# Hybrid block of a two-model kernel: convolution turns moved into the projection, first tap on ScalarE, last heads transposed inside the output product, half of the gate's SiLU folded into an eviction

## The reference, cut to what matters

```python
def hybrid_mixer(h, w_in, conv_w, conv_b, dt_bias, a_log, d_skip, ssm_norm_g, fox_b_f, w_out):
    z, xbc, dt_raw, q, k, v, f_raw = jnp.split(h @ w_in, offs, axis=-1)   # 1024 | 1536 | 16 | 3 x 1024 | 8
    xbc = jax.nn.silu(causal_conv(xbc, conv_w, conv_b))                   # 4 taps, depthwise
    xs, bm, cm = jnp.split(xbc, [D_SSM, D_SSM + SSM_GROUPS * SSM_STATE], axis=-1)
    dt = jax.nn.softplus(dt_raw + dt_bias)
    y = ssd_chunked(xh, dt, -exp(a_log), bm, cm) + d_skip * xh            # 16 heads of 64
    y = y * jax.nn.silu(z)                                                # the gate
    y = y * lax.rsqrt(mean(y * y over each half of 512) + eps) * ssm_norm_g
    o = forgetting_attention(q, k, v, log_sigmoid(f_raw + fox_b_f))       # 8 heads of 128
    return jnp.concatenate([y, o], axis=-1) @ w_out                       # 2048 x 1024
```

## Time and profile before

| | |
|---|---|
| median of 3 runs | 1807.49 us (1804.84 to 1807.61) |
| the profiled execution, own time | 1804.47 us |
| its span in the profile | 1802.7 us |
| TensorE matmul busy | 1724.8 us (96%), 10448 instructions |
| VectorE busy | 1142.3 us (63%) |
| ScalarE busy | 907.1 us (50%) |
| mean granted TensorE clock | 0.98 of full speed |
| hybrid block in the span | about 895 to 1136 us |

### The profile page before, as it was taken

The page is one execution under the profiler, slowest core; times in us unless marked ns, Lnnn a source line. Parts: engine busy times, 40 slices in busy tenths (PEclk is TensorE's granted clock), DMA queues, the critical chain, the costliest instruction groups (busy, mean ns, idle before and its releaser), DMA issues. The chain is left out here.

```text
span 1802.7 us, 24492 instructions
## 1 busy us (share of the span) xinstructions
PE 1724.8 (96%) x10448; PEld 1424.2 (79%) x10448; DVE 1142.3 (63%) x1551; ACT 907.1 (50%) x1137; POOL 11.8 (1%) x25
## 2 busy tenths in 40 slices
PE   8899899998999999999999999999999999989998
PEld 7677688887867887888887777888888888768886
DVE  5786876667868767555666456754565556865554
ACT  5553544455344446443546644644464456954443
POOL 0000000000000000000000000000000000000000
PEclk9899999998999999999999998999999999999999
DMA  7222345442223554555544223655555555345553
GB/s 265 103 95 95 131 145 191 175 164 96 95 102 144 186 187 175 189 187 185 202 161 144 102 103 120 226 186 185 205 189 193 185 198 201 140 139 193 184 176 138
DMA packets 41597, 291.75 MB, mean 162 GB/s; under 512 B 4656, under 2 KB 4912, under 8 KB 7312
## 3 DMA queue, kind: packets, MB, share of 16 engines
q1 hardware_dynamic: 38880, 280.23, 43.3%
q0 software_dynamic: 2608, 9.96, 1.6%
HBM read 289.12 MB, written 1.05 MB: 161 GB/s over the span
## 5 line engine op out<-in xcount | busy, mean ns | idle before, releaser
L468 PE MATMUL pg<-wh,hTh 128*128 128x512 f32 (+1 forms) x2160 | 854.0, 395 | 23.2 <-DVE wl L1807 10.0
L1807 DVE TENSOR_TENSOR wl<-raw,wh 128x2048 fp32r<-128x2048 f32 x259 | 591.9, 2291 | 404.2 <-ACT wh L1242 401.7
L469 PE MATMUL pg<-wl,hTh 128*128 128x512 f32 (+1 forms) x2160 | 834.6, 386 | 0.0
L470 PE MATMUL pg<-wh,hTl 128*128 128x512 f32 (+1 forms) x2160 | 834.2, 386 | 0.0
L1242 ACT ACTIVATE wh<-raw 128x2048 fp32r<-128x2048 f32 x265 | 505.8, 1913 | 304.4 <-DMA raw<-weights 299.8
L468 PEld LDWEIGHTS pg<-wh,hTh 128*128 128x128 f32 x2160 | 410.5, 190 | 112.9 <-issue 16.7
L470 PEld LDWEIGHTS pg<-wh,hTl 128*128 128x128 f32 x2160 | 410.0, 190 | 82.6
L469 PEld LDWEIGHTS pg<-wl,hTh 128*128 128x128 f32 x2160 | 410.9, 190 | 74.9
L1333 ACT ACTIVATE arena<-pg,sm 128x512 f32<-128x512 f32 (+1 forms) x47 | 31.5, 669 | 191.1 <-PE pg L470 191.1
L2445 DVE SCALAR_TENSOR_TENSOR arena<-pg,sm,arena 128x512 f32<-128x512 f32 (+1 forms) x48 | 31.7, 702 | 33.9 <-PE pg L470 33.9
L1289 ACT ACTIVATE hTh<-ps 128x512 fp32r<-128x512 f32 x60 | 32.1, 594 | 38.1 <-PE ps L631 32.9
(11 more groups left out here) (375 smaller groups left out, 1147.9 us busy)
## 6 DMA issues: line engine op xcount, KB each, us to landing
raw<-weights SPq DMA_DIRECT2D x266, 1024.0 KB, 4.8
arena<-wide POOLq DMA_DIRECT2D x9, 512.0 KB, 3.6
x<-x_in SPq DMA_DIRECT2D x2, 512.0 KB, 6.3
cst<-const_tables POOLq DMA_DIRECT2D x1, 1024.0 KB, 5.3
plainh<-dist_tables POOLq DMA_DIRECT2D x2, 512.0 KB, 4.9
arena<-gate_mix POOLq DMA_DIRECT2D x1, 1024.0 KB, 6.2
arena<-token_mix POOLq DMA_DIRECT2D x2, 256.0 KB, 3.9
y_out<-x POOLq DMA_DIRECT2D x1, 512.0 KB, 2.9
```

Source lines behind the costliest of these rows:

```text
L468: pe.matmul(dst, lh, rh, start=first, stop=False)
L469: pe.matmul(dst, lh, rl, start=False, stop=False)
L470: return pe.matmul(dst, ll, rh, start=False, stop=last)
L1807: tt(wl[:, slot, :], raw[:, slot, :], wh[:, slot, :], ALU.subtract)\
```

## The change

Four things in the hybrid block:

1. The small product comes after the first projection block, and the first four groups of convolution transposes are issued inside the second and third projection blocks. `gemm`'s argument `inside` becomes a dictionary from (unit, chunk) to a function.
2. The last tap with the bias is made by ScalarE (`first_tap`, Identity with scale and bias), the other three by VectorE (`later_taps`).
3. The prepared chunks are dealt out anew (2, 10, 4, 2, 2, 3, then one for each SSD head but two at h = 8, 4 and 4; TensorE's attention loop keeps 16). ScalarE and VectorE take the last two chunks' work out of head 7.
4. At the end, group 3 of the attention output is turned inside the first output unit; ScalarE splits groups (0, 1), then a weight unit, then (2, 3); the SiLU of z is made for the first 512 columns by itself and for the last 512 as the function of the block's eviction; the gate's product is made by halves.

```diff
+        HYB_BLOCKS[-1] = HYB_BLOCKS[-1][:2] + (ACT.Silu,)
@@ TensorE
-                gemm(D, (512,) * 3, ("evac_act",) * 3, head=True)
+                def turned(g):
+                    def between():
+                        if g % 2 == 0:
+                            pe.wait_ge(sem["evac_act"], st.evacs["evac_act"])
+                        if g == 0:
+                            c.wait("small_read")
+                        if g >= 4:
+                            c.wait("conv_read")
+                        for j in range(2):
+                            for m in range(M):
+                                last = pe.transpose(...)
+                        last.then_inc(sem["conv_tr"], 1)
+                    return between
+                gemm(D, (512,), ("evac_act",), head=True)
                 small_gemm(24)
-                c.wait("small_read")
-                pe.wait_ge(sem["evac_act"], st.evacs["evac_act"])
-                for g in range(6):
-                    if g == 4:
-                        prepare(3)
...
-                prepare(7)
+                gemm(D, (512,) * 2, ("evac_act",) * 2, inside={(1, 1): turned(0), (1, 2): turned(1), (2, 2): turned(2),
+                                                               (3, 0): turned(3)})
+                prepare(2)
+                for g in (4, 5):
+                    turned(g)()
                 prepare(10)
...
-                    prepare(1)
+                    prepare(2 if h == 8 else 1)
...
-                c.wait("fox_read")
-                transpose_groups(o3, (3,), 0)
-                out_halves()
+                def last_heads():
+                    c.wait("fox_read")
+                    transpose_groups(o3, (3,), 0)
+                out_halves(last_heads)          # called in out_half after chunk 1 of the first unit
@@ ScalarE
+                gemm(D, (512,), ("evac_act",), read(0))
                 c.wait("gate_abs")
...
-                for n in (3, 7, 10):
-                    prepare(n)
+                pump(st.used + 4)
+                first_tap(0)
+                first_tap(1)
+                gemm(D, (512,), ("evac_act",), read(1))
+                first_tap(2)
+                first_tap(3)
+                gemm(D, (512,), ("evac_act",), read(2))
+                plan_blocks(HYB_BLOCKS)
+                prepare(2)
+                for g in (4, 5):
+                    first_tap(g)
+                prepare(10)
...
+                    if h < 7:
                         prepare(1)
                         prepare(1)
                 c.wait("fox_done", 2)
-                split_groups(range(4), 0)
+                split_groups((0, 1), 0)
                 pump(st.used + 3)
-                act.wait_ge(sem["evac_act"], st.evacs["evac_act"])
-                act.activation(HYB_Z, HYB_Z, ACT.Silu).then_inc(sem["z_ready"], 1)
-                pump(st.used + 4)
-                c.wait("o_sq")
+                split_groups((2, 3), 0)
+                act.activation(z3[:, :, 0:512], z3[:, :, 0:512], ACT.Silu).then_inc(sem["z_ready"], 1)
+                prepare(2)
+                pump(st.used + 3)
+                # squares: o_sq is waited for ahead of each half
@@ VectorE
+                pump(st.used + 4)
+                later_taps(0)
+                later_taps(1)
+                gemm(D, (512,), ("evac_act",))
+                later_taps(2)
+                pump(st.used + 4)
+                later_taps(3)
+                gemm(D, (512,), ("evac_act",))
+                prepare(2)
+                for g in (4, 5):
+                    later_taps(g)
...
+                        if h < 7:
                             prepare(1)
                             prepare(1)
                 c.wait("probs_t", 2)
-                split_groups((0, 1), 0)
+                split_groups((0,), 0)
                 fox_read(7)
+                split_groups((1,), 0)
+                pump(st.used + 3)
                 split_groups((2, 3), 0)
+                c.wait("z_ready")
+                c.sig(tt(xs3[:, :, 0:512], xs3[:, :, 0:512], z3[:, :, 0:512], ALU.mult), "o_sq")
+                prepare(2)
+                dve.wait_ge(sem["evac_act"], st.evacs["evac_act"])
+                c.sig(tt(xs3[:, :, 512:D], xs3[:, :, 512:D], z3[:, :, 512:D], ALU.mult), "o_sq")
                 pump(st.used + 3)
```

More of the change, by code:

```diff
@@ L564, in gemm @@
                                 last.then_inc(sem["unit_used"], 1)
-                            if inside and units_done == inside[0] and i == inside[1]:
-                                inside[2]()
+                            if inside and (units_done, i) in inside:
+                                inside[units_done, i]()
                         st.used += 1
@@ L993, in hybrid @@
                 last.then_inc(sem["gram_done"], 1)
-                prepare(2)
+                prepare(3)
                 c.wait("cb_ready")
@@ L1021, in hybrid @@
                         last.then_inc(sem["feat_tr"], 1)
-                    prepare(2)
+                    prepare(4)
                 c.wait("feat_read", 4)
@@ L1069, in out_halves, with out_half @@
                     st.block += 1
-            def out_half(pair, half_, chunk0, turn):
+            def out_half(pair, half_, chunk0, turn, early=None):
                 for u in range(2):
@@ L1080, in out_half @@
                                             half_ == 1 and k == KD - 1)
+                        if early and k == 1:
+                            early()
                     last.then_inc(sem["unit_used"], 1)
@@ L1617, in hybrid, with read, first_tap @@
                 raw3 = V(0, 3072).rearrange("p (m f) -> p m f", m=M)
-                gemm(D, (512,) * 3, ("evac_act",) * 3,
-                     lambda i, pair, w: read_pair(raw3[:, :, 512 * i:512 * i + 512], pair, ACT.Copy))
-                plan_blocks(HYB_BLOCKS)
+                def read(b):
+                    return lambda i, pair, w: read_pair(raw3[:, :, 512 * b:512 * b + 512], pair, ACT.Copy)
+                def first_tap(g):
+                    act.wait_ge(sem["conv_tr"], 3 * DEPTH + g + 1)
+                    for k in (2 * g, 2 * g + 1):
+                        last = act.activation(V(3072 + S * k, S), ps[:, g % 4, (k % 2) * S:(k % 2 + 1) * S], ACT.Identity,
+                                              scale=spar("conv")[:, 36 + k:37 + k], bias=spar("conv_b")[:, k:k + 1])
+                    last.then_inc(sem["conv_first"], 1)
+                gemm(D, (512,), ("evac_act",), read(0))
                 c.wait("gate_abs")
@@ L1635, in hybrid @@
                 last.then_inc(sem["back_read"], 1)
-                for n in (4, 1, 1, 2):
+                for n in (4, 2, 2, 3):
                     prepare(n)
@@ L2474, in hybrid, with later_taps @@
                 stt(SEXP, SAB, -1.0, SAB, ALU.mult, ALU.max).then_inc(sem["gate_abs"], 1)
-                w, b = spar("conv"), spar("conv_b")
+                w = spar("conv")
                 cv = V(3072, 3072).rearrange("p (k s) -> p k s", k=12)
-                for g in range(6):
-                    c.wait("conv_tr")
+                def later_taps(g):
+                    c.wait("conv_first")
                     ks = (2 * g, 2 * g + 1)
                     src = {k: ps[:, g % 4, (k % 2) * S:(k % 2 + 1) * S] for k in ks}
-                    for k in ks:
-                        last = ts(cv[:, k, :], src[k], w[:, 36 + k:37 + k], b[:, k:k + 1], ALU.mult, ALU.add)
-                    c.step(last)
                     for tap in (2, 1, 0):
```

49 lines of the change are left out of this document (20 added, 29 removed).

## The result

| | before | after |
|---|---|---|
| median | 1807.49 us (5 runs, 1804.84 to 1810.38) | 1788.13 us (5 runs, 1787.67 to 1796.52) |
| profiled execution | 1804.47 us, span 1802.7 | 1796.03 us, span 1793.9 |
| from the block's last transposes of x (line 615, now 616) to y's transposes | 895.74 to 1108.86, 213.1 us | 895.70 to 1101.14, 205.4 us |

The ratio is 0.9905 with a 95% interval of 0.988 to 0.9929: a gain of 1%, clear of no change. The median lies 2.4 us under the low end of the predicted range. The two readings differ: 8.4 us gained by the profiled executions, 19.4 us by the medians. The five times of the changed kernel are 1787.67, 1787.96, 1788.13, 1796.03 and 1796.52; the profile is of one near 1796. One median of so few runs says little about such a kernel, so it was run again beside the experiments.

The account below looks back on a forecast made before the run. TensorE, busy 1724.8 of 1802.7 us, was taken to set the end. Gains of 16.3 us less costs of 4.6 gave net 11.7: 1792.8 us for the profiled execution, 1795.8 for the median, range 1790.5 to 1802.0.

Parts of the forecast that it names:

- head 8: SSD loop: TensorE's 2.3 us wait, a queue on VectorE behind a unit's low part, goes with the chunks dealt anew.
- the term of the clock: Hybrid block: new stops may bring products at 1.2 GHz; cost taken as 0.9 us, bounds -1.7 and 3.4.
- the two new stops: ScalarE's queue makes TensorE wait 1.4 us for the convolution's SiLU and 1.9 us at SSD head 1.
- Small sum: Small product, moved inside the projection: TensorE's wait for VectorE's sum goes, 2.5 us, plus 2.3 us of low clock.
- `wl` 1.2: Projection: TensorE's wait for a weight unit's low part goes, 1.2 us, as VectorE's taps no longer stand before it.
- Turns: Projection: groups of four transposes between products cost 0.1 us each in switching, 0.4 us net, bounds 0 and 0.9.
- The end: Attention loop's end: the 3.35 us wait for `fox_read(5)` goes and y's transposes come earlier; 5.5 to 7.5 us, taken as 6.6.
- Front given back: Rival, chance 0.15: new stops at upper ends, 3.0 and 3.3 us, each with a low-clock stretch; 6.2 us gained, 1801.3.
- y late: Rival, chance 0.08: at the end `y_ready` comes 3 us after TensorE asks for it; gain 8.7 us, 1798.8.
- No new stops: Rival, chance 0.10: transfers land earlier and ScalarE is ahead, so no stops are added; 15.9 us gained, 1791.6.
- The stops only move: Rival, chance 0.08: what TensorE no longer waits for is followed by a weight unit late anyway; 1807.5 us.
- Slower by the clock: Rival, chance 0.04: the SiLU stop leaves TensorE at 1.2 GHz and SSD heads' stops keep it there; 40 us give 1815.8.

Follow-up runs that it names:

- the end alone: Former front with the changed end (head 7's last chunks, group 3's turn, gate), against the kernel before: median 1800.05 us, ratio 0.9964.
- the front alone: Changed kernel with the former last attention head, end and gate, against the kernel before: median 1802.3 us, ratio 0.9965.
- the new deal: Changed kernel with prepared chunks 2, 11, 3, 1, 2, 2 before the SSD loop, two at heads 8, 10, 12: median 1788.59 us, ratio 0.9896.
- four parts: Changed kernel with the small product issued in four parts between the second projection block's chunks: median 1789.31 us, ratio 0.9901.
- the version with four parts and new deal: Changed kernel with small product in four parts and prepared chunks dealt otherwise: medians 1786.34 and 1787.00 us, ratios 0.9889 and 0.9882.

## Why the prediction was wrong

What each profile shows: the span from the last transposes of x to y's transposes, and the time at the lower clock in the block (a window of 1 us counts as twice what PEclk lacks to 1; "at" is where the stretch begins).

| profile | whole span | block | low clock, at |
|---|---|---|---|
| before | 1802.7 | 213.1 | 6.8 at 927, 3.4 at 1036, 10.2 at 1084 |
| before, second | 1807.5 | 217.9 | 6.8 at 929, 10.2 at 1007, 3.4 at 1041, 10.2 at 1089 |
| before, third | 1807.4 | 217.9 | 6.8 at 928, 10.2 at 1007, 3.4 at 1041, 10.2 at 1089 |
| after | 1793.9 | 205.4 | 6.8 at 904, 3.4 at 979, 3.4 at 1034, 3.4 at 1082 |
| after, fourth | 1795.1 | 205.5 | 6.8 at 905, 3.4 at 981, 3.4 at 1035, 3.4 at 1083 |
| after, second | 1789.1 | 200.8 | 3.4 at 1029, 3.4 at 1077 |
| after, fifth | 1787.5 | 200.8 | 3.4 at 1027, 3.4 at 1075 |
| after, third | 1783.3 | 199.1 | 3.4 at 1027 |

The same window, just behind the stop of head 8, in the first and the third profile of the kernel before:

```profile
1008.00:1009.00 1.00, 1.00 (x5) 0.79 (x5) 0.00 (x0) 0.64 (x2) 0.00 (x0) 1.00 0.00 0
1008.00:1009.00 1.00, 1.00 (x6) 1.00 (x5) 0.23 (x1) 0.00 (x0) 0.00 (x0) 0.50 0.00 0
```

**The failed step is the term of the clock.** The sign was right, the mechanism of the sum held, and this size was off. Between the two marks the profiles give 216.3 less 202.3 in the mean, 14.0 us, where 11.7 were predicted. The waits give 8.0 of that, against 7.9 predicted. The other 6.0 were predicted as 3.8 (2.3 behind the first stop, 2.8 at the end beyond its waits, less 0.4 for switching and 0.9 for new low stretches). Low time in the block fell from 27.2 us in the mean of three profiles to 10.2 in that of five: 17.0 us, worth 8.5 if TensorE were busy in all of it, which it was not (the earlier trace rows have it idle from 1084 to 1085 with PEclk at 0.81). I priced the clock from a single profile, which lacks the 10.2 us at 1007 that both others have. From its missing I reasoned that the 2.3 us stop at head 8 leaves no low clock; in those two, and in the one with the end alone, it is followed by 10.2 us of it, and with the stop this went too. It makes the blocks of those two 4.8 us longer (217.9 for 213.1). I carried the profiled execution's gain over to the median by adding 3.0 us, as if that distance stayed; it fits a stretch that the change takes away. Averaged over three profiles it is 3.2 us of the 6.0; without it 2.8 are left for the 3.8 predicted, and against the first profile alone the five of the changed kernel gain 10.8 us in the block. The other clock terms were thus a little too kind: in two profiles of five 6.8 us of low clock are still there at the small product, in four of five 3.4 at the end, and the two new stops, charged 0.9 us, drew no low stretch in three profiles and 3.4 us at head 1 in two (0.7 us in the mean).

**What the clock term could not have held** is the rest of the distance to the median: outside the two marks the five profiles are 2.1 us shorter in the mean than the three of before, with no work changed there. The 0.8 ahead looks like chance: the five starts of the block range from 893.0 to 896.8 us, with waits ahead of it of 41.0 to 45.0. Of the 1.3 behind 1.0 is steady (692.8 us in four profiles, 693.7 to 693.8 in all three of before); the other has 691.2, with one stretch of low clock fewer. And the first five runs of the changed kernel happened to be three near 1788 and two near 1796, so the first median of 1788.13 is in part luck. The median of all 19 is 1791.2 us: 4.6 under the forecast, 3.1 over the first median, and within the range. So the range was too narrow rather than in the wrong place: its low end allowed for no new stops, but not for stops as forecast with a kinder clock.

**The front.** Small sum: 2.5 us gone, as forecast. What it left behind: in the first profile of the kernel before the clock falls at 927.6, 0.1 us after the small product ends, in the other two 1.3 us after it. In the changed kernel, with no stop after it, it still fell in two profiles of five, in the middle of the small product. So part of the 2.3 us that I put down to the stop may belong to the row of narrow products ahead of it. `wl` 1.2, line 991 0.9, head 8 2.3, first mask 0.5: all gone. Turns: four transposes at 918.88 hold the next product back 0.36 us, and that product takes 0.09 more than a wide one after its like; the sixteen at 1101.14 take 1.66 until the next product, 0.42 for four. Switching costs some 0.03 us a group, at my lower bound of nothing, where I took 0.1.

**The new stops.** SiLU 1.36 us for 1.4 forecast: the transfer landed at 943.86, and the queue behind it is the one that was added up. The SiLU starts 1.29 us after its table load begins; by the Trainium skill (ScalarE: Activation LUTs, What ACT_TABLE_LOAD costs), which counts a drain beside the load, the stop would have been 2.8 us. The trace again disagrees. Head 1: 1.43 us for 1.9.

**The first tap.** It costs nothing (12 of 0.56 us on ScalarE). That it removes the `wl` wait is refuted: with the tap on VectorE that wait stays away. It is absent too where only the small product came early, so it doesn't need the turns; more was not separated.

**The end.** In the first profile, from the point where the 3.35 us wait began, has 29.1 us to y's transposes, and I forecast 22.5. The new trace has 23.5 (1077.63, the end of the eight transposes, to 1101.14), with 3.4 us at the lower clock in it, which cost 1.7. Without those it would be 21.8. Head 7's two chunks are the largest piece (3 to 4 us), as the 3.3 us that came back show; turning group 3 inside the unit gave nothing. y was ready: VectorE's scaling ends at 1100.1, no wait at 1101.14. The third unit's low part was 0.46 us late; my own times had it 0.3 us late (ready at 1095.9, wanted at 1095.6), and I put nothing for it into the sum.

**The rivals.** Front given back: no, the stops are at 1.4 and the front alone gains 6.3 us. y late: no. No new stops: they came, and that its 15.9 us lies next to the 15.4 us gained by means is luck. It had priced them, with their clock, at 15.9 - 11.7 = 4.2 us, and the new deal that takes them away gave 3.3 and 3.1. The stops only move: not here, but the kernel with the small product early alone shows how near it was, 1.0025. Slower by the clock: the clock went the other way.

The Trainium skill (TensorE: Matmul & The Clock Gate, Part 1: The HAM clock gate) says that the monitor behind the clock runs freely and does not start with the kernel, so that the point of a change varies between executions. The traces agree: the block's waits are the same within 0.1 us in the five profiles, and yet its clock falls at 905 in two of them and not in three. That this is the reason is not shown.

What stays open: why the clock falls in some executions and not in others; why the stretches at 905 and 980 came together (both or neither in every profile of the changed kernel); whether four parts remove the first, make it rarer or do nothing to it; the steady 1.0 us behind the marks, where two stretches of 187.7 us now take 187.4 each; and why waits ahead of the block differ by up to 4 us between executions of one program.

## What to carry to other kernels

In this block a wait could be priced from one profile to a few tenths of a microsecond; the low clock could not, since the same program shows it in some executions and not in others. Several profiled executions are needed to price it, and it wants its own width in the range. When taking a stop out, find out who is next in each queue: the early small product alone moved the stop and cost 4 us, together with the turns inside the projection it paid. Compare means of many runs where the executions of a kernel spread wider than the effect, and beside them one stretch between fixed marks in profiles with the same low clock: that showed 0.4 us where the means showed nothing.

## What the runs showed of the hardware

Without any wait, TensorE's clock fell from 2.4 to 1.2 GHz in the middle of 32 products of 24 and 48 columns in a row (3.5 us at full clock), at 904.7 us in one profile of the changed kernel and at 905.9 in another, and not in three; with the front alone, a different kernel with the same small product, it fell at 905 as well. The pitch of one product went from 0.11 to 0.21 us, and the 6.8 us that followed ran at half speed. The groups of four transposes inside the projection were not followed by a fall in any profile.

A stop of 1.4 us at 978 was followed by 3.4 us of low clock where the clock had fallen at 905 before, and by none where it had not. The stop of 1.6 us for v's last block was followed by 3.4 us of low clock in all eight profiles of the two kernels, and by none in one profile of the version with four parts and new deal. The same program on the same chip took 1785.4 and 1797.2 us: the block's clock made 6.4 us of that with the same waits, waits ahead of the block 3.8, the clock behind it 1.6.
